# From the second perceptron on: moving rows at 128 modulo 256 in a partition instead of at 192

## The chip, the cores and the metric

The kernel runs on one core of one Trainium2 chip. The metric is the device time of one execution in microseconds, the median of the runs shown. The profile is one further execution, whose own time stands beside its span.

## The reference, cut to what matters

Two blocks work on one sequence of 512 tokens of width 1024; 16 meta tokens stand ahead of it in the first block (528 tokens).

```
first_block:  h = concat(meta, x)                          # 528 tokens
  layer 0:    u = rmsnorm(h); z = u @ w_in
              h += concat(hgrn2 scan, block-causal attention) @ w_out
              h += relu(rmsnorm(h) @ w_up)**2 @ w_down     # first perceptron
  layer 1:    h += multiscale_pool(rmsnorm(h)) * scale
              h += relu(rmsnorm(h) @ w_up)**2 @ w_down     # second perceptron
second_block: proj = rmsnorm(h) @ gdn_w_in                 # 512 tokens
              y = concat(gated_delta_rule(...), memory_attention(...)) @ w_out
              h += rmsnorm(y)
              g, u = split(rmsnorm(h) @ w_ffn_in)
              h += rmsnorm((silu(g) * u) @ w_ffn_out)
```

Everything is float32.

## The kernel before, in words

Activations lie with their features on the 128 partitions and the tokens along a partition, so a tensor of 1024 features by 512 tokens is `[128, 8, 512]`: eight rows of 2048 bytes in each partition. A weight block is 128x128.

**The product.** A float32 product is made of three matmuls in the format fp32r (`passes`, L722): the weight's high part by the input's high part, the high part by the input's rest, the weight's rest by the input's high part. The names say it: `whi`/`wlo` are the weight's parts, `UH`/`UL`, `USH`/`USL`, `KFH`/`KFL`, `MFH`/`MFL`, `TH`/`TL`, `MTH`/`MTL`, `FH`/`FL`, `YH`/`YL` are inputs. Three such matmuls are called a triple here. In every matmul the weight block is loaded first (LDWEIGHTS), while the matmul before it runs, and the input row (the moving row) then streams through.

**The stages**, in order: the projections of layer 0 from `UH`/`UL` with rows of 528 tokens, in two halves of 264; the first perceptron from `UH`, its turned inputs `KTH` and its hidden rows `KFH`; memory and pool products; from about 750 us the second perceptron from `USH`/`USL` (512 tokens), hidden rows `MFH`, turned inputs `MTH`; the input projection `gin` from `USH`/`USL` (the weight's rest is in `rlo` there); the delta rule and the memory attention; the output projection from `YH`, `OMH`; the last perceptron from `USH`, `FH` and `TH`. The up-projections of both 512-token perceptrons and the down-projection of the last one are partly made of products over 256 tokens (seven products for eight), which is where the 256-column matmuls come from.

**What sets the order.** TensorE's program is written out by hand. SyncE's queue loads weight slots (`raw`, eight blocks each, four buffers, or pairs of slots); ScalarE rounds each to `whi`, VectorE subtracts to get `wlo`; semaphores count slots (`w_lo`), tiles (`tile_done`) and evacuations (`evac`). In the second perceptron some of the down-projection's weights land in a free part of the input's own buffer (`USLF<-W`).

**Where things lie.** `place` hands out SBUF addresses one behind the other, from 16512 on; `region` lays tensors one behind the other from a given start. The places of a row's first byte in its partition, modulo 256, follow from the code:

- `raw`, `whi`, `wlo` are multiples of 4096 from 16512 on: 16512 is 128 modulo 256, and block rows are 512 bytes, so every weight row begins at 128 (128 modulo 512 too).
- `u_at` (L292) is 82560, 128 modulo 256. `UH` and `UL` begin there. Their rows are 528x4 = 2112 bytes, so row k begins 64k further, its second half 32 more: the eight places 0, 32, ..., 224 come in turn.
- `us_at` (L296) is `u_at + 320` = 82880: `USH` and `USL` (L449) begin at 192. Their rows are 2048 bytes, so all begin at 192.
- `S0` (L309) is 134080: 192. All that `region` lays from `S0` in rows of 2048 or 1024 bytes begins at 192: `MFH`, `MFL`, `MTH`, `MTL`, `TH`, `TL`, `FH`, `FL`, `YH`, `YL`, `OML`, `QKV`. The hidden rows `KFH` of the first perceptron start there too, but are 2112 bytes long and go through all eight places.
- `OMH`, `MH`, `ML` and the turned rows `KTH` are laid from the end of the memory: 160 for the first row.

Of the kernel before, what the change touches and what calls it, by code (L numbers as in the profile page):

```python
# [259 lines left out]
def build(nc, xT, memT, W, vecs_d, masks_d, rope_d, gates_d, out):  # L260
    ctx = ExitStack()
    with ctx:
        arena = ctx.enter_context(nc.sbuf_tensor("arena", [P, 212000 // 4], F32))
        base = [16512]
# [7 lines left out]
        def place(name, shape, dt):  # L272
            t, end = at(name, shape, dt, base[0])
            base[0] = (end + 31) // 32 * 32
            return t

        def region(start, *items):

            got, off = [], start
            for name, shape, dt in items:  # L280
                t, end = at(name, shape, dt, off)
                off = (end + 31) // 32 * 32
                got.append(t)
            return got
# [7 lines left out]
        u_at = base[0]  # L292
        scratch = u_at - NB * 2 * SLOT * P * 4 - KT * L * 4
        UH = place("UH", [P, KT, L], FR)
        UL = place("UL", [P, KT, L], FR)
        us_at = u_at + 320  # L296
        assert us_at + 2 * KT * SEQ * 4 <= u_at + 2 * KT * L * 4
        R = [place(f"R{c}", [P, L], F32) for c in range(2)]
        SQ = [place(f"SQ{c}", [P, L], F32) for c in range(2)]
# [6 lines left out]
        masks = place("masks", [P, LEVELS + 5, P], F32)  # L306
        zero = place("zero", [P, 1], F32)
        eps = place("eps", [P, 1], F32)
        S0 = base[0]  # L309
        level = masks[:, 0:LEVELS, :]  # L310
        turn = masks[0:ROPE, LEVELS, 0:ROPE]
        ident = masks[:, LEVELS + 1, :]
# [5 lines left out]
        ZH, KN, QRX, KRX, VT, KR, TAB, SR0, SR1, KSQ, SN, stat = region(  # L318
            S0, ("ZH", [P, 16, L], F32), ("KN", [P, HEADS, L], F32), ("QRX", [ROPE + 4, HEADS, L], F32),
            ("KRX", [ROPE + 4, HEADS, L], F32), ("VT", [P, 5, 512], F32), ("KR", [ROPE, L], F32),  # L320
            ("TAB", [ROPE, 2, L], F32), ("SR0", [ROPE, L], F32), ("SR1", [ROPE, L], F32), ("KSQ", [ROPE, L], F32),
            ("SN", [ROPE, L], F32), ("stat", [P, 16], F32))
        QR, KRS = QRX[0:ROPE, :, :], KRX[0:ROPE, :, :]
        hw = S0 + 16 * L * 4
        CHI, CLO = region(S0 + 8 * L * 4, ("CHI", [P, 4, L], FR), ("CLO", [P, 4, L], FR))
        CZ, = region(hw + 8 * L * 4, ("CZ", [P, 4, L], F32))
# [21 lines left out]
        HH, HL, RL0, RL1, SB0, SB1 = region(  # L348
            S0, ("HH", [P, 8, L], FR), ("HL", [P, 8, L], FR), ("RL0", [P, L], F32), ("RL1", [P, L], F32),
            ("SB0", [P, L], F32), ("SB1", [P, L], F32))  # L350
        RL, SB, TD = [RL0, RL1], [SB0, SB1], [SB0, SB1]


        UV, WR, RC = region(S0, ("UV", [P, POOL_CHUNKS, D], F32), ("WR", [P, POOL_CHUNKS, 4, POOL_STEP], F32),
                            ("RC", [P, 8], F32))
# [10 lines left out]
        windows, = region(AB0 - 3 * 8192 - 1024 - 4096, ("windows_m", [P, 4, POOL_STEP], F32))  # L366
        MEM, = region(S0 + 20 * L * 4, ("MEM", [P, KT, NMEM], F32))
        MSQ, RM = region(S0 + 12 * L * 4, ("MSQ", [P, KT, NMEM], F32), ("RM", [P, NMEM], F32))
# [3985 lines left out]
```

## Time and profile before

| | us |
|---|---|
| median of 3 runs | 1866.42 (1862.13 to 1869.57) |
| the profiled execution's own time | 1862.51 |
| its span, first to last instruction | 1860.4 |
| TensorE busy | 1817.1 (98%) |
| weight loads busy | 1658.4 (89%) |
| VectorE busy | 1308.8 (70%) |
| ScalarE busy | 925.1 (50%) |

Matmuls are pipelined: in the timeline each lasts longer than the distance to the start of the next one. So the time that a matmul takes from the span is the distance between starts (called the step below), and not its duration. The granted clock was 1.0 of 2.4 GHz in nearly the whole span (mean 0.996).

### The profile page before, as it was taken

To read this page: it belongs to the slowest core of one execution; us is meant where nothing else is said; L and a number is where in the kernel's file an instruction comes from. 1 tells how busy PE (TensorE), PEld (TensorE's weight loads), DVE (VectorE), ACT (ScalarE), POOL (GpSimd) and SP (SyncE) were. 2 spreads that over 40 slices of the span, in tenths; PEclk is the share of its full clock that TensorE was granted. 3 is DMA by queue.
4 is the path that set the end of the run, shared out by engine and by line. 5 is a ranking of instruction groups with operands and counts; after the bars stand their busy time and mean duration, and the time that the engine had idled before them with its cause. 6 is when DMAs were issued, how large, how long until landed. Compare 5 with 4: busy or idle time off the path is not lost.

```text
span 1860.4 us, 31132 instructions
## 1 busy us (share of the span) xinstructions
PE 1817.1 (98%) x12498; PEld 1658.4 (89%) x12498; DVE 1308.8 (70%) x1882; ACT 925.1 (50%) x1557; POOL 33.1 (2%) x31
## 2 busy tenths in 40 slices
PE   7999999999999999999999999999999999999997
PEld 7888878999999999898899878787889898999996
DVE  4664476767777776877777768778738379877775
ACT  5456444544334446654344433645667464544553
POOL 0100001200000000000000000000000000000000
PEclk9999999999999999999999999999999999999998
DMA  5211101232233232333233322222200422333331
GB/s 198 71 57 58 60 1 46 80 100 94 91 92 113 80 119 89 105 102 103 91 104 105 103 97 92 80 69 80 80 1 33 139 80 91 114 103 102 109 108 56
DMA packets 63364, 162.55 MB, mean 87 GB/s; under 512 B 4632, under 2 KB 29464, under 8 KB 63096
## 3 DMA queue, kind: packets, MB, share of 16 engines
q1 hardware_dynamic: 62368, 158.59, 25.9%
q8 instruction: 99, 1.62, 0.4%
q10 hardware_dynamic: 856, 2.00, 0.3%
q14 instruction: 41, 0.34, 0.1%
HBM read 156.38 MB, written 4.19 MB: 86 GB/s over the span
## 4 chain that ended last, share of the span: by engine, by line
PE 86%; DVE 7%; ACT 3%; DMA 2%; DVEq 1%; issue 1%; SPq 0%; ACTq 0%
PE ps L722 73%; PE ps L1405 2%; DMA USLF<-W 1%; PE ps L945 1%; PE ps L1425 1%; DVE wlo L3400 1%; PE ps L1274 1%; DVE wlo L3030 1%; PE ps L920 0%; PE ps L1410 0%; PE ps L1253 0%; PE ps L1251 0%; ACT WU L2638 0%; DMA H<-xT 0%; PE ps L921 0%
## 5 line engine op out<-in xcount | busy, mean ns | idle before, releaser
L722 PE MATMUL ps<-UH,whi 128*128 128x264 f32 (+1 forms) x696 | 202.8, 291 | 9.6 <-DVE wlo L3030 9.6
L722 PE MATMUL ps<-USH,whi 128*128 128x512 f32 (+1 forms) x584 | 209.2, 358 | 0.8 <-DVE USL L3944 0.7
L722 PE MATMUL ps<-USL,whi 128*128 128x512 f32 (+1 forms) x584 | 201.8, 345 | 0.0
L722 PE MATMUL ps<-UL,whi 128*128 128x264 f32 (+1 forms) x696 | 198.1, 285 | 0.0
L722 PE MATMUL ps<-UH,wlo 128*128 128x264 f32 (+1 forms) x696 | 197.7, 284 | 0.0
L1965 ACT ACTIVATE whi<-raw 128x1024 fp32r<-128x1024 f32 x114 | 119.3, 1052 | 83.1 <-PE ps L722 63.1
L722 PE MATMUL ps<-KFH,whi 128*128 128x264 f32 x512 | 145.7, 285 | 1.6 <-DVE KFL L3442 1.5
L722 PE MATMUL ps<-KFH,wlo 128*128 128x264 f32 x512 | 145.3, 284 | 0.0
L722 PE MATMUL ps<-KFL,whi 128*128 128x264 f32 x512 | 145.2, 284 | 0.0
L722 PEld LDWEIGHTS ps<-UH,whi 128*128 128x128 f32 (+1 forms) x696 | 130.9, 188 | 10.9 <-issue 9.8
L722 PE MATMUL ps<-TH,whi 128*128 128x256 f32 x504 | 139.1, 276 | 0.0
L722 PE MATMUL ps<-TL,whi 128*128 128x256 f32 x504 | 139.1, 276 | 0.0
L722 PE MATMUL ps<-TH,wlo 128*128 128x256 f32 x504 | 139.1, 276 | 0.0
L3030 DVE TENSOR_TENSOR wlo<-raw,whi 128x1024 fp32r<-128x1024 f32 x80 | 100.6, 1263 | 45.1 <-ACT whi L1965 35.1
L722 PEld LDWEIGHTS ps<-UL,whi 128*128 128x128 f32 (+1 forms) x696 | 131.1, 188 | 0.6 <-issue 0.2
L722 PEld LDWEIGHTS ps<-UH,wlo 128*128 128x128 f32 (+1 forms) x696 | 130.5, 188 | 0.0
L722 PEld LDWEIGHTS ps<-USH,whi 128*128 128x128 f32 x584 | 109.7, 188 | 16.7 <-issue 3.0
L722 PEld LDWEIGHTS ps<-USL,whi 128*128 128x128 f32 x584 | 109.7, 188 | 16.4 <-issue 2.2
L722 PE MATMUL ps<-USH,rlo 128*128 128x512 f32 x288 | 113.0, 392 | 0.0
L722 PE MATMUL ps<-MFH,whi 128*128 128x512 f32 x256 | 101.4, 396 | 1.4 <-DVE FOM L3462 1.3
L722 PE MATMUL ps<-MFH,wlo 128*128 128x512 f32 x256 | 100.6, 393 | 0.0
L722 PE MATMUL ps<-MFL,whi 128*128 128x512 f32 x256 | 100.3, 392 | 0.0
(588 smaller groups left out, 5079.5 us busy)
## 6 DMA issues: line engine op xcount, KB each, us to landing
raw<-W SPq DMA_DIRECT2D x134, 512.0 KB, 3.5
raw_p<-W SPq DMA_DIRECT2D x46, 1024.0 KB, 5.0
ULF<-W SPq DMA_DIRECT2D x22, 512.0 KB, 4.0
USLF<-W SPq DMA_DIRECT2D x22, 512.0 KB, 4.0
raw_d<-W SPq DMA_DIRECT2D x14, 512.0 KB, 3.9
H<-xT SPq DMA_DIRECT2D x4, 528.0 KB, 6.7
spill<-H SPq DMA_DIRECT2D x1, 2048.0 KB, 7.0
H<-spill SPq DMA_DIRECT2D x1, 2048.0 KB, 8.6
```

Of the source, the lines that this page charges most:

```text
L722: mm = pe.matmul(dst, a, b, start=start and n == 0, stop=stop_ and n == 2, skip_group_check=again)
L945: mm = pe.matmul(ps[:, 4 + l % 2, c * P:(c + 1) * P], columns(a, c), columns(b, c), start=True, stop=True)
L1274: mm = pe.matmul(flat[:, 3584:3584 + n], VT[:, c, h * P:(h + 1) * P], PT[x % 2][:, c, 0:n], start=c == 0, stop=c == j)
L1405: mm = pe.matmul(ps[:, bank, x * P:(x + 1) * P], a(x), b(x), start=True, stop=True)
L1425: pe.matmul(ps[:, bank, :], ones, SQ[y % 2][:, META:L], start=True, stop=True).then_inc(N["l2_sum"], 1)
L1965: act.activation(whi[s % NB][:, :, :], raw[s % NB][:, :, :], ACT.Copy).then_inc(w_hi, 1)
L3030: dve.tensor_tensor((rlo if gin else wlo)[s % NB][:, :, :], raw[s % NB][:, :, :], whi[s % NB][:, :, :].bitcast(F32), ALU.subtract).then_in ...
L3400: dve.tensor_tensor(dst, source, hi_, ALU.subtract).then_inc(w_lo, 1)
```

## The change

`us_at` becomes `u_at`, so `USH`, `USL`, `USF`, `USLF` begin 320 bytes lower, at 128 modulo 256. `S0` becomes 192 bytes higher, so all that is laid from it moves by 192 bytes, from 192 to 128 modulo 256 (the rows of `KFH` and the like go through the same eight places, begun elsewhere). What is laid from the end of the memory does not move. No instruction, order, wait, size or transfer is added or taken away.

```
-        us_at = u_at + 320
+        us_at = u_at + 0
         assert us_at + 2 * KT * SEQ * 4 <= u_at + 2 * KT * L * 4
...
-        S0 = base[0]
+        S0 = base[0] + 192
```

## Rows read from the trace of the kernel before

**Rows 1.** The page's shares of the engines, and TensorE's granted clock in 40 slices.
```profile
PE 1817.1 (98%) x12498; PEld 1658.4 (89%) x12498; DVE 1308.8 (70%) x1882; ACT 925.1 (50%) x1557; POOL 33.1 (2%) x31
...
PEclk9999999999999999999999999999999999999998
```

**Rows 2.** The page's chain that ended last: shares of the span by line.
```profile
PE ps L722 73%; PE ps L1405 2%; DMA USLF<-W 1%; PE ps L945 1%; PE ps L1425 1%; DVE wlo L3400 1%; PE ps L1274 1%; DVE wlo L3030 1%; PE ps L920 0%; PE ps L1410 0%; PE ps L1253 0%; PE ps L1251 0%; ACT WU L2638 0%; DMA H<-xT 0%; PE ps L921 0%
```

**Rows 3.** Stretches: stretch, length, then busy us (instructions) of PE, PEld, DVE, ACT, POOL.
```profile
1110.00:1330.00 220.00, 220.00 (x1015) 177.55 (x1014) 170.44 (x258) 104.55 (x163) 1.11 (x2) 1.00 0.24 80
...
1555.00:1850.00 295.00, 292.56 (x2074) 271.74 (x2075) 229.72 (x314) 147.51 (x220) 0.00 (x0) 1.00 0.28 95
```

**Rows 4.** Groups of TensorE by shape: count | busy us, mean duration ns | idle before.
```profile
L722 PE MATMUL ps<-USH,whi 128*128 128x512 f32 x352 | 143.9, 409 | 0.0
L722 PE MATMUL ps<-TH,whi 128*128 128x256 f32 x504 | 139.1, 276 | 0.0
...
L722 PE MATMUL ps<-MFH,whi 128*128 128x512 f32 x256 | 101.4, 396 | 1.4 <-DVE FOM L3462 1.3
...
L722 PE MATMUL ps<-USH,whi 128*128 128x256 f32 x232 | 65.4, 282 | 0.8 <-DVE USL L3944 0.7
...
L722 PE MATMUL ps<-FH,whi 128*128 128x512 f32 x164 | 63.9, 389 | 1.1 <-DVE FL L3990 1.1
...
L722 PE MATMUL ps<-MTH,whi 128*128 128x256 f32 x224 | 62.3, 278 | 0.0
...
L722 PE MATMUL ps<-YH,whi 128*128 128x256 f32 x64 | 18.1, 284 | 0.0
```

**Rows 5.** Timeline (start us, duration us, instruction): first and last of 252 TH matmuls.
```profile
1594.14 0.28 PE L722 MATMUL ps<-TH,whi 128*128 128x256 f32 x1
...
1622.59 0.28 PE L722 MATMUL ps<-TH,wlo 128*128 128x256 f32 x1
```

**Rows 6.** Timeline: 36 MTH matmuls and their follower, in two pairs.
```profile
811.59 0.28 PE L722 MATMUL ps<-MTH,whi 128*128 128x256 f32 x1
...
815.67 0.28 PE L722 MATMUL ps<-USH,whi 128*128 128x256 f32 x1
...
847.32 0.28 PE L722 MATMUL ps<-MTH,whi 128*128 128x256 f32 x1
...
851.56 0.28 PE L722 MATMUL ps<-USH,whi 128*128 128x256 f32 x1
```

**Rows 7.** Timeline: 21 matmuls of 512 columns and their follower, then 189 and theirs.
```profile
788.57 0.40 PE L722 MATMUL ps<-MFH,whi 128*128 128x512 f32 x1
...
793.47 0.28 PE L722 MATMUL ps<-USH,whi 128*128 128x256 f32 x1
...
1117.39 0.39 PE L722 MATMUL ps<-USH,whi 128*128 128x512 f32 x1
...
1160.65 0.59 PE L1425 MATMUL ps<-SQ,masks 128*128 128x512 f32 x1
```

**Rows 8.** Timeline: the first matmuls of consecutive half rows of UH, 264 columns.
```profile
30.77 0.28 PE L722 MATMUL ps<-UH,whi 128*128 128x264 f32 x1
...
31.13 0.28 PE L722 MATMUL ps<-UH,whi 128*128 128x264 f32 x1
...
31.49 0.29 PE L722 MATMUL ps<-UH,whi 128*128 128x264 f32 x1
...
31.86 0.28 PE L722 MATMUL ps<-UH,whi 128*128 128x264 f32 x1
```

**Rows 9.** VectorE lines: count, duration ns min/median/max, first and last start.
```profile
L3002 DVE SCALAR_TENSOR_TENSOR UL<-H,vecs,UH x24: 758/762/770, 5.6 to 714.8; 128x528 fp32r<-128x528 f32 x24
...
L2999 DVE SCALAR_TENSOR_TENSOR USL<-H,vecs,USH x16: 744/746/748, 736.5 to 1103.6; 128x512 fp32r<-128x512 f32 x16
```

**Rows 10.** Transfers: count, KB each, median us from issue to landing.
```profile
ULF<-W SPq DMA_DIRECT2D x22, 512.0 KB, 4.0
USLF<-W SPq DMA_DIRECT2D x22, 512.0 KB, 4.0
```

## The prediction

> **What bounds the kernel now.** I read the engines' shares first: TensorE is busy 98% of the span at full granted clock [rows 1]. The chain of waits then says of what kind the path is: 73% of it is line L722, the triples [rows 2]. The table by stretches shows that this holds where the moved rows are used: from 1110 to 1330 us TensorE is busy 220.00 of 220 us, from 1555 to 1850 us 292.56 of 295 [rows 3]. So a nanosecond more or less per matmul goes nearly whole into the time, and nothing else in the kernel hides it. All other engines stand below 75% and are not moved in time.
>
> What a matmul costs is its step, the distance between starts. In 252 matmuls over `TH` it is (1622.59 - 1594.14) / 251 = 0.1133 us for 256 columns [rows 5]. Two pairs of the second perceptron run the same 36 instructions over the same rows at the same places: once 4.08 / 36 = 0.1133, once 4.24 / 36 = 0.1178 us [rows 6]. For 512 columns there are two speeds as well: 4.90 / 21 = 0.2333, and 43.26 / 189 = 0.2289 us [rows 7]. At 2.4 GHz the columns alone would take 0.1067 and 0.2133 us. So some 7 to 20 ns of each step are not columns, and the stream settles in one of several rhythms, in which it stays for hundreds of matmuls. A rhythm can be entered or missed without any change of place: the two pairs differ only in what came before. This share of the step is all that the change can touch.
>
> **The change part by part.** Nothing is added or removed: 12498 matmuls, all transfers, all waits stay. What moves is the place of rows.
>
> How many triples read a moved row from about 750 us on [rows 4]: of 512 columns 352 over `USH` (with `rlo` among them for the rest), 256 over `MFH`, 164 over `FH`, and 32 over `YH` from the code, in all 804. Of 256 columns 504 over `TH`, 224 over `MTH`, 232 over `USH`, 64 over `YH`, and 24 over `FH` from the code, in all 1048. Their share of the time is 804 x 3 x 0.2289 = 552 us and 1048 x 3 x 0.1153 = 363 us (0.1153 is between the two speeds), 915 us together, about half of the span.
>
> Bounds, from the two speeds. One triple of 256 columns differs by 3 x (117.8 - 113.3) = 13.4 ns between its rhythms, one of 512 columns by 3 x (233.3 - 228.9) = 13.2 ns. In the trace all 504 `TH` triples are quick (mean duration 276 [rows 4]), 4 of the 14 pairs of the second perceptron are (each with 16 triples over `MTH` and 16 over `USH`), and 21 of 24 of `FH`; the rest of the 1048, about 400, are slow. Of the 512-column triples nearly all are in the quicker of their two.
> - Downward: the 400 slow triples become quick, 400 x 13.4 ns = 5.4 us. For 512 columns the trace has no quicker rhythm, but `TH` has less per column: 113.3 x 2 = 226.6 against 228.9 ns, 7 ns per triple, 804 x 7 = 5.6 us. Together -11 us.
> - Upward: the 650 quick triples of 256 columns become slow, 650 x 13.4 = 8.7 us, and the 804 of 512 columns fall into their slower rhythm, 804 x 13.2 = 10.6 us. Together +19 us.
>
> Which value. The only rows that show both places with a weight at 128 beside them are the 264-column triples over `UH`, whose rows go through all eight places. By the layout the triple that begins at 30.77 us reads at 128, the next at 160, the next at 192: they take 0.36, 0.36 and 0.37 us [rows 8]. So with rows of 264 columns a place of 128, the weights' own, costs no more than one of 192, and perhaps up to 10 ns less per triple. There the places change with every triple and no rhythm settles, so it says little about which rhythm a uniform place at 128 would find. If half of the least printed difference, 5 ns, held for a fifth of the 1852 triples, it would be 2 us. I take -2 us, nearest to these rows, and keep -11 and +19 as the ends.
>
> The engines beside it. VectorE's subtraction over rows at four different places takes 758 to 770 ns for 528 columns, over rows all at 192 it takes 744 to 748 ns for 512 [rows 9]: per column 1.44 to 1.46 and 1.45 to 1.46. So places in steps of 64 bytes cost VectorE nothing. Transfers into `ULF` (places 160, 224, 32, 96) and into `USLF` (192) both land in a median of 4.0 us [rows 10]; four of the latter are on the path around 870 to 945 us as a wait of the weights (1% of the chain [rows 2]), and if the new place changed one by 5%, it would be under 1 us in all. I take both at zero: the bound is +-1 us.
>
> The first perceptron's hidden rows go through the same eight places in another order, 512 triples. Their neighbours stay the same, only the phase at the first one shifts. Zero, with a bound of 512 x 1 ns = 0.5 us either way.
>
> Here a rule can be weighed. The trace shows that identical instructions over identical places take 113.3 or 117.8 ns [rows 6], and that a step of 512 columns stands 15.6 ns above its columns [rows 7]. The Trainium skill, "TensorE: Matmul & The Clock Gate", section "Step-by-step: what each phase is for", says that the moving row and the weight load have a read port each, so that a load takes nothing from the running matmul. By that rule the relation of the two places is of no account and the change would give 0. The same page's section "Back-to-back issue gap" gives an isolated matmul N/2.4 + 2.5 ns; by it an undisturbed step would be 215.8 and 109.2 ns, and were it reached everywhere, 804 x 39 + 1048 x 18 ns = some 50 us would go. No run of this trace of 512 fp32r columns comes near it, so I give that little weight.
>
> Sum: the profiled execution took 1862.5 us (span 1860.4 and 2.1 around it); with -2 it is 1860.5. The median of the runs shown is 1866.4, 3.9 above the profiled one, with a spread of 7 us among three, which may itself be rhythms won and lost. On the median's scale the forecast is 1864 us.
>
> **The rivals.**
> (a) Forecast, no change that a measurement can tell (0.5% of the time, 9 us, is about what one can): the rhythms belong to rows of equal place and lengths of 256 and 512 columns and not to where the place is; some pairs change theirs, with little net. For it: rows 6 and 7 show that one place has both speeds. 1864 us. Chance 0.44.
> (b) Slower: the weight row and the moving row in the same place. The load of the next weights starts with the matmul; if both then ask for the same part of the memory at once, the matmul must yield at each line. Its place is every one of the 1852 triples, its price the slower rhythm, up to +19 us: 1885 us. It decides against (a) once about half of them fall into it. For it: all `TH` triples now are at the quick step and can only lose, and so is what they are worth, 504 x 13.4 = 6.8 us. Against it: the triple at 128 in rows 8 is not slower than its neighbours. Chance 0.28.
> (c) Faster: at 192 the moving row runs 64 bytes ahead of the weights and meets them; at 128 it does not. Then the slow pairs and the 512-column triples gain, -11 us or somewhat more: 1855 us, and further down if the 512-column step has a quicker rhythm than the trace shows. For it: 0.36 against 0.37 us in rows 8, and that the 512-column step is above twice the quick 256-column one. Chance 0.28, of which less than a third is below 1850.
> (d) The change doesn't do what it says: `OMH`, `MH`, `ML` and `KTH` stay at 160, as 24 + 64 + 224 triples. That is little beside 1852 and changes no forecast; it is within (a).
>
> **How the numbers follow.** The likeliest case gives 1864 us. The range takes in (a), most of (b) up to its whole price, and (c) with a part of what lies beyond its bound: 1847 to 1884 us. Faster by over 0.5% is (c), 0.28; slower by over 0.5% is (b), 0.28; the rest is 0.44. The forecast's own range is 1857 to 1873.
>
> **What would show it right or wrong.** Right: the timeline of `TH` at 0.1133 us a step, pairs of the second perceptron partly at 0.1133 and partly at 0.1178, 512 columns at 0.229. (b) would show `TH` at a mean duration of 279 to 280 instead of 276, and 512-column groups at 397 or more. (c) would show `MTH` and `USH` of 256 columns at 276 throughout and the 512-column groups below 388. VectorE's and the transfers' rows should stay as they are. A step outside all the values named, in particular a 512-column step under 225 or over 234 ns, would say that the place matters more than any row of this trace can show, and that would make the prediction wrong in its bounds.

## The result and the profile after

The changed kernel takes 1874.55 us (median of 7 runs, 1871.41 to 1876.52), the kernel before, run beside it, 1867.42 us (7 runs, 1862.13 to 1870.90). The ratio is 1.0037, with a 95% interval of 1.0022 to 1.0052: slower, by 7 us. The forecast was 1864 us, 2 us faster. The profiled execution after took 1875.45 us (span 1873.4, granted clock 0.996 as before), 13.0 us more in span than the profiled one before, which was among the quickest of its kernel. What separates these two numbers, 7 and 13, is told below with the runs of the kernel before.

The page's shares of the engines, after; they answer to [rows 1]:
```profile
PE 1829.8 (98%) x12498; PEld 1675.0 (89%) x12498; DVE 1309.6 (70%) x1882; ACT 925.4 (49%) x1557; POOL 33.3 (2%) x31
```
The same instructions, and TensorE busy for 12.7 us more. The weight loads, which are TensorE's too, are busy for 16.6 us more; VectorE, ScalarE and GpSimd moved by less than 1 us each, and no new wait appears. The groups by shape, after, to be laid beside [rows 4] (count, then busy us, mean duration in ns, then idle us before them):
```profile
L722 PE MATMUL ps<-USH,whi 128*128 128x512 f32 x352 | 142.9, 406 | 0.0
L722 PE MATMUL ps<-TH,whi 128*128 128x256 f32 x504 | 142.5, 283 | 0.0
...
L722 PE MATMUL ps<-MFH,whi 128*128 128x512 f32 x256 | 101.1, 395 | 0.9 <-DVE FOM L3462 0.4
...
L722 PE MATMUL ps<-USH,whi 128*128 128x256 f32 x232 | 66.3, 286 | 0.7 <-DVE USL L3944 0.6
...
L722 PE MATMUL ps<-FH,whi 128*128 128x512 f32 x164 | 64.2, 392 | 1.1 <-DVE FL L3990 1.1
...
L722 PE MATMUL ps<-MTH,whi 128*128 128x256 f32 x224 | 63.4, 283 | 0.0
...
L722 PE MATMUL ps<-YH,whi 128*128 128x256 f32 x64 | 18.4, 287 | 0.0
```
Every group of 256 columns is up (`TH` 276 to 283 ns, `MTH` 278 to 283), while of 512 columns `USH` and `MFH` are a little down and `FH` is up (389 to 392 ns), although its steps fall like those of the others (below). Durations overlap and hide size and even sign, so the distance between starts has to be read. The timeline after, first and 241st of a run of `TH` matmuls, as [rows 5]:
```profile
1599.17 0.28 PE L722 MATMUL ps<-TH,whi 128*128 128x256 f32 x1
...
1627.97 0.28 PE L722 MATMUL ps<-TH,whi 128*128 128x256 f32 x1
```
28.80 / 240 = 0.1200 us a step, a value that no row of before has, and by the prediction's own sign one outside its bounds. 512 columns, the first of 180 and what follows them, as the second part of [rows 7]:
```profile
1122.28 0.39 PE L722 MATMUL ps<-USH,whi 128*128 128x512 f32 x1
...
1163.08 1.02 PE L1425 MATMUL ps<-SQ,masks 128*128 128x512 f32 x2
```
40.80 / 180 = 0.2267 us a step: quicker than both speeds of before. The steps of the two lengths went opposite ways.

Joined instruction by instruction, the two profiles differ so: the runs over `TH` and `TL` +10.0 us, `MTH` +2.3, `USH` of 256 columns +2.2, `YH` and `FH` of 256 +0.6, together +15.0 us at 256 columns; at 512 columns `MFH` -2.0, `USH` -1.5, `FH` -0.7, `YH` -0.3, together -4.5 us. The part before 745 us has +1.1, the rest of the kernel about +1.4. Sum: 13.0 us.

One more view shows who is late. One tile's instructions after (count, duration in ns min/median/max, first and last start), loads and matmuls of `TH`, then the loads of `MTH` and those of `rlo` beside 512 columns:
```profile
L722 PEld LDWEIGHTS ps<-TH,whi x504: 187/192/192, 1567.5 to 1825.1; 128*128 128x128 f32 x168
L722 PE MATMUL ps<-TH,whi x504: 277/283/283, 1567.7 to 1825.2; 128*128 128x256 f32 x168
...
L722 PEld LDWEIGHTS ps<-MTH,whi x224: 192/192/192, 797.0 to 1057.0; 128*128 128x128 f32 x112
...
L722 PEld LDWEIGHTS ps<-USH,rlo x288: 187/188/188, 1109.9 to 1344.9; 128*128 128x128 f32 x144
```
and `TH` before:
```profile
L722 PEld LDWEIGHTS ps<-TH,whi x504: 187/188/188, 1563.9 to 1811.9; 128*128 128x128 f32 x168
L722 PE MATMUL ps<-TH,whi x504: 276/276/276, 1564.1 to 1812.0; 128*128 128x256 f32 x168
```
Beside 256 columns a weight load is recorded 4 ns longer, beside 512 it is not. This goes with distance 0 (defined below) and not with slow steps as such: in e11 (below), whose steps of 256 columns are as slow, three in four loads over `TH` have 187 or 188 ns, and in f3, in the slower rhythm of before, all have. Vector and transfer rows stand as in [rows 9] and [rows 10]:
```profile
L2999 DVE SCALAR_TENSOR_TENSOR USL<-H,vecs,USH x16: 743/746/749, 737.6 to 1106.4; 128x512 fp32r<-128x512 f32 x16
...
ULF<-W SPq DMA_DIRECT2D x22, 512.0 KB, 4.0
USLF<-W SPq DMA_DIRECT2D x22, 512.0 KB, 4.0
```

### The profile page after: what moved, and what is told of

The parts are those of the page before. It is cut to its first block, busy times and chain, and to the rows that moved or that the text cites. A ratio compares the mean times of both kernels' runs of the same rounds, so it can differ in the third digit from the quotient of the medians.

```text
span 1873.4 us, 31132 instructions
## 1 busy us (share of the span) xinstructions
PE 1829.8 (98%) x12498; PEld 1675.0 (89%) x12498; DVE 1309.6 (70%) x1882; ACT 925.4 (49%) x1557; POOL 33.3 (2%) x31
## 4 chain that ended last, share of the span: by engine, by line
PE 87%; DVE 6%; ACT 3%; DVEq 1%; DMA 1%; issue 1%; ACTq 0%; SPq 0%
PE ps L722 74%; PE ps L1405 2%; DMA USLF<-W 1%; PE ps L945 1%; DVE wlo L3400 1%; PE ps L1425 1%; PE ps L1274 1%; DVE wlo L3030 1%; PE ps L920 0%; PE ps L1253 0%; PE ps L1410 0%; PE ps L1251 0%; PE ps L1349 0%; ACT WU L2638 0%; PE ps L921 0%
## 5 line engine op out<-in xcount | busy, mean ns | idle before, releaser
L722 PE MATMUL ps<-UH,whi 128*128 128x264 f32 (+1 forms) x696 | 202.9, 291 | 10.5 <-DVE wlo L3030 10.5
```

Of the source, the lines that this page charges most:

```text
L722: mm = pe.matmul(dst, a, b, start=start and n == 0, stop=stop_ and n == 2, skip_group_check=again)
```

## The experiments

"Distance" is the place of the moving row minus that of the weight row, modulo 256: 64 before, 0 after.

**One half of the change each.** e1 takes only the first edit, e2 only the second.
```
e1:  -  us_at = u_at + 320        e2:  -  S0 = base[0]
     +  us_at = u_at + 0               +  S0 = base[0] + 192
```


> Only USH and USL move to 128 modulo 256; all that is laid from S0 stays at 192. Theory P (the place of the row decides the step of its own matmul): steps over USH and USL become 0.1200 us at 256 columns and 0.2267 at 512, as after the change, while TH stays at 0.1133, MTH at 0.1133 or 0.1178 and MFH and FH at 0.2289. The sum from the two traces: 352 triples of 512 columns gain 6.7 ns each (2.3 us), 232 of 256 columns lose about 9 ns each (2.1 us): within 1 us of before. Rival N (the change's loss is no matter of place but of noise or of the first part's phase): the steps of TH and MTH move too, or USH does not.

> Only what is laid from S0 moves to 128; USH and USL stay at 192. Theory P: TH 0.1200 (504 triples lose 20 ns each, 10.1 us), MTH 0.1200 (224 lose about 10 each, 2.2 us), YH 0.1200 (0.4 us), MFH, FH and YH of 512 columns at 0.2267 (452 triples gain 6.7 ns each, 3.0 us); USH as before. Net about +9.5 us against before, more than the whole change's +7 to +10. Rival N: less than +4 us, since no one part carries the loss.

e1: 1867.76 us, ratio 1.0024 (1.0005 to 1.0043). By shape:
```profile
L722 PE MATMUL ps<-USH,whi 128*128 128x512 f32 x352 | 143.0, 406 | 0.0
L722 PE MATMUL ps<-TH,whi 128*128 128x256 f32 x504 | 139.1, 276 | 0.0
...
L722 PE MATMUL ps<-USH,whi 128*128 128x256 f32 x232 | 66.3, 286 | 0.8 <-DVE USL L3944 0.7
```
e2: 1873.27 us, ratio 1.0053 (1.0033 to 1.0074). By shape:
```profile
L722 PE MATMUL ps<-USH,whi 128*128 128x512 f32 x352 | 144.0, 409 | 0.0
L722 PE MATMUL ps<-TH,whi 128*128 128x256 f32 x504 | 142.6, 283 | 0.0
...
L722 PE MATMUL ps<-USH,whi 128*128 128x256 f32 x232 | 65.7, 283 | 0.7 <-DVE USL L3944 0.6
```
Each group follows its own place: in e1 only `USH` has the steps of after (0.1200 and 0.2267), in e2 only the groups laid from `S0`. One thing beside that: `MTH` and `USH` of 256 columns take turns in the stream, and in these two profiles the one that did not move has none of the quick steps of 0.1133 that it had in part of before (0.9 us each). That may be chance, as their number differs between executions of before too (f1 to f3). Most of the loss is `TH`'s (+10.0 us in e2), and `USH` alone nearly pays for itself (+2.2 and -1.5 us in the steps). e1's measured +4.3 us is more than that 0.7, and the steps of its profiled run (1865.10 us) don't explain it. Five of its ten runs lie at 1863.0 to 1865.6 and five at 1869.9 to 1875.8; the upper five may have `TH` in the slower rhythm that is told of below, which was not profiled.

**Place or distance.** e3 moves the rows to place 0 (distance 128). e4 moves the weights to 192 and the rows to 0, so that all places differ from before and the distance does not. e7 is e4 with `USH` at 192, distance 0 for it alone, at a place that before was at distance 64.
```
e3:  us_at = u_at + 128    S0 = base[0] + 64
e4:  base = [16576] (was [16512], rlo and raw_p too)    us_at = u_at + 64
e7:  as e4, but us_at = u_at + 0
```


> All moved rows at 0 modulo 256, weights at 128 as before. It asks whether 128 is bad because the weights lie there (theory R: the distance from the weight row decides; a distance of 128 should then be at least as good as the 64 of before, with TH at 0.1133 and no 0.1200 anywhere, and the time at or below before's), or whether every place but 192 gives the step of 0.1200 at 256 columns (rival: 192 is special; time about +10 us).

> Weight rows at 192 and moved rows at 0 modulo 256: both 64 higher than before, so their distance is what it was (64), but the places are other ones. Theory R (distance decides): the steps of before, TH 0.1133, MTH 0.1133 or 0.1178, 512 columns 0.2289, and the time within 0.2% of before. Rival A (the absolute place of the moving row decides): the steps are those of the run with the rows at 0 and the weights at 128, whatever these are.

> Weight rows at 192; USH and USL at 192 too (distance 0), and all that is laid from S0 at 0 (distance 64). Theory R: USH and USL take 0.1200 at 256 columns and 0.2267 at 512, the values that the change gave at place 128, although their place is now the one of before; TH 0.1133 or 0.1178, MFH and FH 0.2289. Rival A (the absolute place decides): USH and USL as before, 0.1133 or 0.1178 and 0.2289.

e3: 1879.86 us, ratio 1.0085 (1.0064 to 1.0106): `TH` 0.1187, 512 columns 0.2320 to 0.2333. e4: 1863.91 us, ratio 1.0001 (0.9986 to 1.0015). e7: 1867.06 us, one run. e3's expectation failed: a distance of 128 is not as good as 64 but costs 16 us, at both lengths. The rival beside it, that only place 192 is good, falls with e4. The tile `TH` in e4:
```profile
L722 PEld LDWEIGHTS ps<-TH,whi x504: 187/187/188, 1564.7 to 1819.4; 128*128 128x128 f32 x168
L722 PE MATMUL ps<-TH,whi x504: 279/279/279, 1564.9 to 1819.6; 128*128 128x256 f32 x168
```
By shape in e7:
```profile
L722 PE MATMUL ps<-USH,whi 128*128 128x512 f32 x352 | 142.9, 406 | 0.0
L722 PE MATMUL ps<-TH,whi 128*128 128x256 f32 x504 | 139.1, 276 | 0.0
...
L722 PE MATMUL ps<-USH,whi 128*128 128x256 f32 x232 | 66.3, 286 | 0.9 <-DVE USL L3944 0.8
```
With the weights and all rows of these groups moved, e4 has the steps and the time of before; its profiled run has `TH` in the slower of before's two rhythms. e7's `USH` has 286 and 406 ns, to the nanosecond what after has, though it stands at 192. The distance decides, and not where in the 256 bytes the row stands. That it counts modulo 256 is borne out at one point: modulo 512, `USH` lies 320 from the weights in before and 64 in e4, with the same steps. It is not modulo 128, as 0 and 128 differ.

**Other distances.** e5: rows at 64 (distance 192), e6: at 160 (32), e11: at 224 (96).
```
e5:  us_at = u_at + 192  S0 = base[0] + 128
e6:  us_at = u_at + 32   S0 = base[0] + 224
e11: us_at = u_at + 96   S0 = base[0] + 32
```


> All moved rows at 64 modulo 256, weights at 128: the distance from the weight row is 192, the one multiple of 64 not seen yet. Theory R (the distance decides, and the step has a few fixed values for each) gives no value for it beforehand; from the three known distances the triple of 256 columns should lie in 340 to 360 ns and that of 512 in 680 to 706, the time between 1858 and 1880 us. A theory in which only 0 (the same place) is bad at 256 columns would give TH at 0.1133 to 0.1178; the run with the rows at 0 already speaks against it.

> All moved rows at 160 modulo 256, weights at 128: distance 32, half way between the change's 0 and before's 64. If the step changes smoothly with the distance, TH lies between 0.1133 and 0.1200 and 512 columns between 0.2267 and 0.2289, and the time between 1863 and 1875 us. Rival: half lines cost their own, since a row then begins in the middle of a 64-byte piece; then both steps are above those of the neighbours (the 264-column triples whose row begins at an odd multiple of 32 took 363 to 367 ns in the trace of before, against 361 to 364 at even ones, with 224 as the exception) and the time is above 1875 us.

> All moved rows at 224 modulo 256, weights at 128: distance 96. In the 264-column rows of the first part, whose place changes with each triple, this place had the quickest triples of the eight (357 to 359 ns against 361 to 367). If what they show carried over to rows of one place, this would be the best place of all, with a time under 1860 us. Theory R with fixed rhythms for each distance says that these rows tell nothing of it; from the distances seen the time is then between 1862 and 1880 us.

e5: 1875.43 us, ratio 1.0040 (1.0017 to 1.0063). e6: 1876.02 us, 1.0052 (1.0030 to 1.0074). e11: 1885.53 us, 1.0096 (1.0064 to 1.0127). By shape in e11, then `MTH` in e5:
```profile
L722 PE MATMUL ps<-USH,whi 128*128 128x512 f32 x352 | 145.4, 413 | 0.0
L722 PE MATMUL ps<-TH,whi 128*128 128x256 f32 x504 | 142.5, 283 | 0.0
```
```profile
L722 PE MATMUL ps<-MTH,whi x224: 276/276/281, 796.0 to 1052.9; 128*128 128x256 f32 x112
```
Median steps in us, a third of the distance between the starts of triples:

| distance | kernels | `TH`, 256 | 512 columns |
|---|---|---|---|
| 0 | after | 0.1200 | 0.2267 |
| 32 | e6 | 0.1167 | 0.2333 |
| 64 | before, e4 | 0.1133 or 0.1177 | 0.2290 |
| 96 | e11 | 0.1193 to 0.1207 | 0.2333 |
| 128 | e3 | 0.1187 | 0.2320 to 0.2333 |
| 192 | e5 | 0.1177 | 0.2327 to 0.2333 |

At distance 192 both rhythms of distance 64 come back: in e5 `TH` is at 0.1177, but 127 of the 224 triples over `MTH` are at 0.1133. So e5 loses at 512 columns and hardly at 256. e6 fits neither of its answers: `TH` lies between its neighbours as a smooth change would have it, while 512 columns are slower than at 0 and at 64 and the time is above 1875 us, as its rival would have it.

e11 was chosen because the 264-column rows of the first part are quickest when they pass 224; if such rows told the speed of a uniform place, it had to fall below 1860 us. It is the slowest by its time (with e3 by the ratio, whose intervals overlap). What the prediction took its value from, a reading of rows whose places change with each triple, does not carry over.

**Is it the load?** e9 is after, e10 before, with all but one in eight of the weight loads over `TH` and `TL` cut to half their columns. The matmul then also works with 64 of 128 weight columns, so load and matmul are halved together. Outputs 64 to 127 of that product lack these terms; the moved rows, their number and their places stay.
```
+  m = P if first and k == 0 else 64
-  mm = passes(ps[:, bank, 0:NMEM], whi[v % NB][:, 4 * half + k, :], ...
+  mm = passes(ps[0:m, bank, 0:NMEM], whi[v % NB][:, 4 * half + k, 0:m], ...
```


> The kernel after the change, with one part of the computation left out: in the products over TH only the first block of each sum is loaded and multiplied with all 128 weight columns, all others with the first 64 (their outputs 64 to 127 lack those terms). The load of the next weights is half as long; moving rows and their places stay. Theory L (at distance 0 the load is what is delayed, and at 256 columns the load is long enough to set the step: its recorded duration went from 188 to 192 ns there): TH's steps with a half load fall from 0.1200 to 0.1133 or less. Rival M (the moving row itself is delayed by its place): they stay at 0.1200.

> The same halving of the weight load in the kernel before (rows at 192, distance 64), with the same part left out. Theory L: nothing is delayed by the load in the quick rhythm, so TH stays at 0.1133, or falls a little to the columns' own 0.1067 plus a fixed part; it can't be above 0.1178. Rival M: no difference to the kernel before. If both kernels come to the same step with a half load, the loss of the change at 256 columns is in the overlap of the load with the row.

The timeline of e9 where half loads (`128*64`) and whole ones (`128*128`) stand side by side:
```profile
1603.72 0.28 PE L722 MATMUL ps<-TH,whi 128*64 128x256 f32 x1
1603.83 0.28 PE L722 MATMUL ps<-TL,whi 128*64 128x256 f32 x1
1603.94 0.28 PE L722 MATMUL ps<-TH,wlo 128*64 128x256 f32 x1
1604.06 0.28 PE L722 MATMUL ps<-TH,whi 128*128 128x256 f32 x1
1604.18 0.28 PE L722 MATMUL ps<-TL,whi 128*128 128x256 f32 x1
1604.30 0.28 PE L722 MATMUL ps<-TH,wlo 128*128 128x256 f32 x1
1604.41 0.28 PE L722 MATMUL ps<-TH,whi 128*64 128x256 f32 x1
```
`TH` in e10:
```profile
L722 PE MATMUL ps<-TH,whi x504: 275/276/282, 1563.4 to 1811.6; 128*64 128x256 f32 x150, 128*128 128x256 f32 x18
```
In e9 the half triple from 1603.72 to 1604.06 takes 0.34 us. By the trace's own starts in ns, 378 of the 504 triples take 339 to 340; a triple with whole weights steps 119, 120 and 117 ns, and the half triple behind it still 116 to 117 a step. `MTH` and `USH` of 256 columns, whose loads are untouched, stay at 0.1200. e9 took 1863.44 us, e10 1861.65 (one run each; before 1869.25 beside them). e10's `TH` steps 0.1133 too. So at distance 0 and 256 columns the loss goes with whole weights: with half of their columns the place costs nothing, 6.7 ns less a step there, against none from before's quicker rhythm. That it is the load and not the matmul's own width is likely, since the load is what reads the weight rows whose distance counts, but e9 halves both and can't part them. Nor is it simply the load that begins beside a row: the last half matmul ahead of a whole triple, beside which the first whole load begins, still steps 0.1135 (mean of 39 cases), and the first slow step is that of the matmul whose own weights are whole.

From e9 comes an estimate of the load's length too: its recorded duration fell from 188 to 134 ns, so 64 weight columns are worth some 54 ns and 128 some 108. That is nearly all of a 256-column step and less than half of a 512-column one.

**What a mixture is worth.** e8 puts the long rows of the `S0` part (`FH`, `MFH`) at distance 0 and leaves `TH`, `MTH` and `USH` at 64. e12 lets only gin read its 512-column rows, `USH` of m > 3, from a region of its own at 128, and the small `ABH` product beside them.
```
e8:  f_at = S0 + 2 * 7 * 4 * NMEM * 4 + 192        (FH0, FL0, ...; MFH's region at S0 + 192)
e12: UGH, UGL = region(u_at, ("UGH", [P, KT, SEQ], FR), ("UGL", [P, KT, SEQ], FR))
     (written for m > 3 in place of USH, USL; read at L1661 and L1384)
```


> Each length at the distance that suits it: MFH, MFL, FH, FL (512 columns, 420 triples) at 128, the weights' place; TH, TL, MTH, MTL (256 columns) and USH, USL, YH, YL at 192 as before. Theory R: 420 x 6.7 ns = 2.8 us less for the 512 columns, nothing lost at TH if it keeps the rhythm of 0.1133: -2.8 us, ratio 0.9985. If TH enters the slower rhythm of 0.1178 instead, +6.7 us on top, ratio 1.002. If the rival is right that the change's loss came from something other than the 256-column steps, the time is nearer to the change's, ratio 1.003 or more.

> Only the input of gin (288 triples of 512 columns, no 256-column product near it, not at the end of a stage that TH follows) moves to 128; all else is as before. Theory R: 288 x 6.7 ns = 1.9 us less, ratio 0.999; the 256-column products keep their two rhythms. Rival: a change of the phase in gin upsets the rhythm of TH later, as in the mix (+6.7 us): ratio 1.002 or more.

e8: 1869.94 us, ratio 1.0015 (1.0000 to 1.0029). Its long rows step 0.2267, but `TH` is at 0.1177 throughout. By shape, a few lines further down in its file:
```profile
L725 PE MATMUL ps<-TH,whi 128*128 128x256 f32 x504 | 141.2, 280 | 0.0
...
L725 PE MATMUL ps<-FH,whi 128*128 128x512 f32 x164 | 64.4, 393 | 1.1 <-DVE FL L3993 1.1
```
504 x 3 x 4.4 ns = 6.7 us over the quicker rhythm, more than the long rows give back. But `TH` is there in f2, f3 and e4 as well, where no long row was moved. e12: 1867.36 us, ratio 0.9988 (0.9968 to 1.0009), the best version I found and not distinguishable from before. Its gain by steps is 288 x 3 x 2.3 ns = 2 us; its profiled run has `TH` at 0.1177.

**The kernel before, three times more.** If `TH` can take either rhythm at distance 64, the runs of one program must show both.

> The kernel before, unchanged, profiled once more. Theory T (the rhythm of TH decides the cluster): a profiled execution of 1860 to 1865 us has TH at a mean duration of 276 (step 0.1133), one of 1868 to 1872 us has TH at 279 to 280 (step 0.1178). Rival: the cluster is decided elsewhere (the first 745 us, the stalls at stage ends), and TH is at 276 in both.

> As the run before it: the kernel before once more, so that both clusters are likely to be among the profiles. The same two answers.

> As the two runs before it: the kernel before a third time. The same two answers.

They took 1866.15, 1867.85 and 1869.88 us. The tile `TH` in f1, then in f2, then in f3, last `MTH` in f2:
```profile
L722 PE MATMUL ps<-TH,whi x504: 276/276/276, 1567.9 to 1815.9; 128*128 128x256 f32 x168
```
```profile
L722 PE MATMUL ps<-TH,whi x504: 279/279/283, 1562.5 to 1817.3; 128*128 128x256 f32 x168
```
```profile
L722 PE MATMUL ps<-TH,whi x504: 279/279/279, 1564.7 to 1819.4; 128*128 128x256 f32 x168
```
```profile
L722 PE MATMUL ps<-MTH,whi x224: 276/276/280, 796.0 to 1051.9; 128*128 128x256 f32 x112
```
From first to last start f1 needs 248.0 us, f2 254.8, f3 254.7: the same program, 6.7 us apart by the rhythm of one tile's stream. That is the largest single difference among the profiles of before, but it does not decide the time alone. Only f3 is as expected; f1 (quick) and f2 (slow) lie outside the two bands that were named, and only 1.7 us apart. f2 wins back 2.1 us in `MTH` and `USH`, where 127 of 224 `MTH` triples are at 0.1133 against 32 in f1, and f1 loses time elsewhere. It lies 3.6 us above the profiled run of before: 2.3 of them are there at 745 us, 0.9 are in `MTH` and `USH`, and 1.6 in eight `KM` matmuls that step 0.427 instead of 0.216 us, as the granted clock falls to its lower level, 1.2 GHz (0.53 of full on average from 1359 to 1362 us, with TensorE busy all through the 5 us before); `MFH` gives 1.2 back.

It is also the likely reason why the profiles differ by 13 us and the medians by 7; the runs behind the medians were not profiled. After, nearly all of `TH` is at 0.1200 (489 of 504 triples): by the sum of its steps 10.0 us above the quicker rhythm, in which before was profiled, but only 3.2 above the other one.

## Why the prediction was wrong

- **What bounds the kernel**: held. 10.5 of the 13.0 us are steps over the moved rows, and nothing hid them. It says that all other engines stand below 75%, but passes over the weight loads at 89% [rows 1], on which rival (b) and e9 turn.
- **The number of moved triples**: held (804 and 1048). With the third rhythm, 504 x 3 x 6.7 ns gives 10.1 us for `TH`, and 10.0 was found.
- **"Which value", -2 us from [rows 8]**: this step failed, and with it the sign: +7.1 us by the medians, and by steps +15.0 us at 256 columns and -4.5 at 512. It took 264-column rows, whose places change with each triple, for a sign of what a uniform place does. In them 128 is no worse than 192; as a uniform place beside 256 columns it costs 20 ns a triple over the quick rhythm. e11, at the place where those rows are quickest of all, is slower still, 1.0096. The prediction itself said that such rows say little about a rhythm, and chose them still as the nearest.
- **Upward bound**: too low at 256 columns. The upward end let quick triples become as slow as the slower rhythm of before, 13.4 ns a triple. The runs show a third rhythm at distance 0: 20 ns a triple over the quick one, and 7 over the slow one, so that the 400 slow triples lose too: +15.0 us where the bound had 8.7. That the total of +19 held is luck: its other term, +10.6 us at 512 columns, came out as -4.5.
- **Downward bound at 512 columns**: its size held. 226.6 ns was worked out as twice 113.3, and the step is 0.2267; 804 x 7 = 5.6 us against 4.5 found, in part since some triples of 512 columns stand at 0.2300 to 0.2323 after (over 30 of the 256 of `MFH`).
- **Rival (b)**, the same place for both: right in its direction at 256 columns alone, and there, as far as e9 goes, in naming the load; at 512 the same distance is the quickest. Rival (c) was right only there. The prediction gave both lengths one sign. A condition on the length, asking how much of a step the load fills (by the estimate from e9 some 108 of 113 ns against 108 of 227), might have parted them; no run tests it. Why 512 columns gain rather than stay is not explained by that.
- **Engines beside, transfers, first perceptron**: held near zero. The part before 745 us has +1.1 us, 0.8 of it ahead of the first matmul, so the first perceptron stayed within its 0.5.
- **The rule weighed**: the Trainium skill, "TensorE: Matmul & The Clock Gate", "Step-by-step: what each phase is for", has a load take no read bandwidth from the running matmul, and by it the change is worth 0. The runs don't agree: the same instructions step 0.1133 to 0.1207 us by the distance between the two rows, e4 and e7 show that it is the distance, and e9 that at distance 0 the loss is gone with half of the weights' columns. No run shows whether a read port is what is shared.

Shown by runs: that distance decides (e4, e7), that each group goes by its own distance (e1, e2; whether a neighbour's distance takes part in the choice between the two rhythms is open), that at distance 0 and 256 columns the loss is gone with half-wide weights (e9), that one program has two rhythms at distance 64 (f1 to f3). Not shown: what in the memory makes the distance count, whether it is the load or the matmul's width that e9 took the loss from, why distances 64 and 192 have two rhythms where 0 has one, and what picks between them. e8 only shows that `TH` was at 0.1177 after an `FH` stream of another step; whether that stream caused it was not tried by itself. That the memory delays the load is argued from the 4 ns in its record, not shown.

## What to carry to other kernels

Where TensorE is saturated, measure the step, the distance between starts, for each length of moving row. Here short rows (256 columns, about as long as the load by the estimate above) do best 64 bytes off the weights', long ones (512) at the weights' own, of the six distances measured, so one place for all rows is a compromise and each length should be judged apart. Don't read the worth of a uniform place from rows whose place changes with each matmul, and bound an unseen arrangement wider than the rhythms that the trace happens to contain. Before a difference of some 7 us is believed, see which rhythm each profile is in.

## What was not expected of the hardware

A uniform shift of 64 bytes between two operands changes a 256-column step by 6% (0.1133 to 0.1200; 2% from the slower 0.1177) with no change of instruction. At distance 0 a step of 512 columns is exactly two of 0.1133. And identical programs keep one of two rhythms through all of 504 triples, 248.0 or 254.7 us.
